# Memory scan: the state products of a step are issued ahead of its output products

## The reference, cut to what matters

```python
def step(state, inp):
    s, n, m = state
    qc, kc, vc, ic, fc = inp
    ...
    qk = jnp.einsum('bhtd,bhsd->bhts', qc, kc) * jnp.exp(dmat - m_t[..., None])
    num = jnp.einsum('bhts,bhsv->bhtv', qk, vc) + w_inter[..., None] * jnp.einsum('bhtd,bhdv->bhtv', qc, s)
    den = jnp.sum(qk, axis=-1) + w_inter * jnp.einsum('bhtd,bhd->bht', qc, n)
    h = num / jnp.maximum(jnp.abs(den), jnp.exp(-m_t))[..., None]
    ...
    kw = kc * jnp.exp(g - m_new[..., None])[..., None]
    s_new = decay[..., None, None] * s + jnp.einsum('bhsd,bhsv->bhdv', kw, vc)
    n_new = decay[..., None] * n + jnp.sum(kw, axis=2)
    return (s_new, n_new, m_new), h
```

## Time and profile before

| | us |
|---|---|
| median of 3 runs | 4023.66 (4020.28 to 4027.84) |
| profiled execution, its time | 4025.71 |
| profiled execution, its span | 4023.7 |
| PE busy | 3649.3 (91% of the span) |
| PEld busy | 2898.3 (72%) |
| DVE busy | 2201.8 (55%) |
| ACT busy | 1558.4 (39%) |
| POOL busy | 1129.1 (28%) |

### The profile page before, as it was taken

The page is one execution under the profiler, slowest core; times in us unless marked ns, Lnnn a source line. Parts: engine busy times, 40 slices in busy tenths (PEclk is TensorE's granted clock), DMA queues, the critical chain, the costliest instruction groups (busy, mean ns, idle before and its releaser), DMA issues. The chain is left out here.

```text
span 4023.7 us, 43905 instructions
## 1 busy us (share of the span) xinstructions
PE 3649.3 (91%) x16690; PEld 2898.3 (72%) x16690; DVE 2201.8 (55%) x2454; ACT 1558.4 (39%) x2064; POOL 1129.1 (28%) x593
## 2 busy tenths in 40 slices
PE   4899997587899999979889899999798999999997
PEld 1778886465687878766677667777676888888886
DVE  7467635655788888856656322222245543353338
ACT  3321233344677777734322222222222333232234
POOL 2231222035211111133331212122143444444443
PEclk8899998788899999969999999999999999999999
DMA  4412135655899999944421312111253323222333
GB/s 158 122 37 75 68 113 168 222 172 200 325 402 398 402 397 402 397 183 157 150 105 53 124 46 69 52 65 61 89 184 139 123 90 99 95 94 97 98 110 126
DMA packets 174817, 650.33 MB, mean 162 GB/s; under 512 B 21376, under 2 KB 55008, under 8 KB 158528
## 3 DMA queue, kind: packets, MB, share of 16 engines
q1 hardware_dynamic: 135424, 555.34, 38.1%
q10 hardware_dynamic: 28864, 60.87, 4.0%
q0 software_dynamic: 10368, 31.91, 2.1%
HBM read 540.71 MB, written 107.34 MB: 161 GB/s over the span
## 5 line engine op out<-in xcount | busy, mean ns | idle before, releaser
L3625 POOL TENSOR_TENSOR t_wl<-t_raw,t_wh 128x1024 fp32r<-128x1024 f32 x160 | 386.4, 2416 | 522.5 <-ACT t_wh L3671 522.3
L100 PE MATMUL m_b<-b_high,m_high 128*128 128x512 f32 x960 | 404.9, 422 | 10.7 <-POOL m_low L2498 8.1
L102 PE MATMUL m_b<-b_high,m_low 128*128 128x512 f32 x960 | 382.1, 398 | 0.0
L101 PE MATMUL m_b<-b_rest,m_high 128*128 128x512 f32 x960 | 381.8, 398 | 0.0
L2496 POOL TENSOR_TENSOR m_high<-m_raw,m_one 128x1024 fp32r<-128x1024 f32 x60 | 120.6, 2010 | 788.5 <-PE m_b L102 723.1
L100 PE MATMUL t_b<-b_high,t_wh 128*128 128x512 f32 x768 | 302.0, 393 | 15.2 <-POOL t_wl L3625 15.2
L102 PE MATMUL t_b<-b_high,t_wl 128*128 128x512 f32 x768 | 299.7, 390 | 0.0
L101 PE MATMUL t_b<-b_rest,t_wh 128*128 128x512 f32 x768 | 299.6, 390 | 0.0
L3671 ACT ACTIVATE t_wh<-t_raw 128x1024 fp32r<-128x1024 f32 x160 | 169.1, 1057 | 312.7 <-PE t_b L102 292.4
L100 PE MATMUL zs_z<-zs_hs,zs_high 128*128 128x512 f32 (+1 forms) x584 | 226.6, 388 | 27.9 <-POOL zs_hs L279 27.9
L100 PEld LDWEIGHTS m_b<-b_high,m_high 128*128 128x128 f32 x960 | 184.8, 193 | 64.4 <-issue 11.3
(11 more groups left out here) (647 smaller groups left out, 8774.4 us busy)
## 6 DMA issues: line engine op xcount, KB each, us to landing
moe_raw<-in_expert_w SPq DMA_DIRECT2D x79, 2048.0 KB, 10.2
ex_raw<-in_expert_w SPq DMA_DIRECT2D x39, 2048.0 KB, 10.7
t_raw<-in_w_ff SPq DMA_DIRECT2D x128, 512.0 KB, 3.4
m_raw<-in_w_ug SPq DMA_DIRECT2D x60, 512.0 KB, 4.6
yrows<-ex_y ACTq DMA_DIRECT2D x38, 512.0 KB, 11.1
zs_raw<-in_ada_w SPq DMA_DIRECT2D x32, 512.0 KB, 4.7
gates<-m_ob SPq DMA_DIRECT2D x32, 512.0 KB, 2.8
me_g<-gates SPq DMA_DIRECT2D x32, 512.0 KB, 4.0
```

The source lines that it names most:

```text
L100: nc.tensor.matmul(out, w[0], x[0], start=first, stop=False)
L101: nc.tensor.matmul(out, w[0], x[1], start=False, stop=False)
L102: return nc.tensor.matmul(out, w[1], x[0], start=False, stop=last)
L3625: self.nc.gpsimd.tensor_tensor(self.wl[u % self.NW][:], self.raw[u % 2][:], self.wh[u % self.NW][:].bitcast(F32), ALU.subtract).then_inc(s ...
```

## The change

In `Memory.tensor` the loop of the 8 state products, with its waits on `kw_done`, moves ahead of the block of the output products. The wait on `updated` stays ahead of both. Nothing is added or removed, and the programs of DVE, ACT, POOL and SP are the same.

```diff
             pe.wait_ge(self.updated, 3 * n)
+            for d in range(2):
+                pe.wait_ge(self.kw_done[d], n + 1)
+                for h, out in enumerate(self.four(self.X[d], self.EX, d)):
+                    mm = mm_(out, self.kw[d][:, h, :], self.v[:, ORDER[d][n], h, :], start=True, stop=True)
+                mm.then_inc(self.stepped, 1)
             if i >= 0:
                 for d in range(2):
                     pe.wait_ge(self.q_in[d], i + 1)
@@
                         mm = mm_(out, self.inter[d][i % 2][:, h, :], self.state[:, d, h, :], start=False, stop=True)
                     mm.then_inc(self.o_done, 1)
-            for d in range(2):
-                pe.wait_ge(self.kw_done[d], n + 1)
-                for h, out in enumerate(self.four(self.X[d], self.EX, d)):
-                    mm = mm_(out, self.kw[d][:, h, :], self.v[:, ORDER[d][n], h, :], start=True, stop=True)
-                mm.then_inc(self.stepped, 1)
             Z.multiply(pe, fills[n][1])
```

## The result

The changed kernel takes 4033.27 us (median of 12 runs, 4029.78 to 4037.76) against 4025.15 us (12 runs, 4020.28 to 4032.62): a ratio of 1.0021, 95% interval 1.0012 to 1.0029. It is slower by 8.1 us, where 6.5 was forecast. That is just at the bound of 0.2%, with the interval on both sides of it; the forecast gave "no change" 0.64 and "slower" 0.32. One profile of each kernel shows the scan more sharply than the times do. In programs with the same code up to there, the starts of steps 2 to 5 repeat to 0.05 us. From step 6 on they don't: there the same code took up to 3 us more or less, mostly by its clock. And the stretch behind the scan, whose code is never changed, took between 3248.7 and 3254.6 us in the fourteen profiles, so the times carry a scatter that has nothing to do with the scan.

A forecast was written before the change was run, and what follows sets the result against it. PE was busy 91% of the span, but the change was priced from the engines' waits in the scan's steps. 0.9 + 1.8 - 2.1 + 5.4 + 0.5 = +6.5 us on the median 4023.66 gave 4030.2, range 4023 to 4037.

The forecast's parts named there:

- The cost is the delay of the last output: Steps with outputs: the last output comes 1.79 us later where PE reached it without a wait; earlier state products help nobody.
- two regimes: Steps 2 to 4 are bound by PE's work, 18.98 us each; from step 5 the chain crosses engines and delays pass on.
- Steps 2 to 4, +0.9: PE's key transposes wait for DVE's late state update, 0.3 us in each of three steps; bounds 0 to 1.5.
- Step 5, +1.8: The output delay of 1.79 us passes undiminished through DVE's mask, ACT's copy, SP's queue and the tile's DMA.
- DVE's idle time in front of L374: Step 5, a sign to look for in the changed kernel's profile: this idle time about 1.8 us longer.
- POOL's price of nothing: Step 5: POOL's splitting holds two other DVE instructions just as long, so the sum is unchanged; bounds -1 and +1.
- Step 6, -2.1: State products fill PE's 3.23 us hole, outputs keep full clock, DVE starts 0.6 us late instead of 2.7; bounds -3.7 to +0.2.
- Steps 7 to 9, +5.4 and 0.5: Three output delays of 1.79 us come through, plus 0.25 us each in steps 7 and 8 for a later clock rise.
- The sum: Whole kernel: all terms together +6.5 us, 4030.2 us against the median, 0.16% slower.
- A: Rival, slower for sure: step 6's outputs stay at half clock and give nothing back; +9.8 us, time 4033.5; chance 0.27.
- C: Rival, faster: DVE's state update waits for the state products, so earlier ones shorten the scan; chance 0.04.
- B: Rival, nearly nothing: step 6 returns 3.7, steps 2 to 4 lose nothing, clock kinder in steps 7 to 9; +2.0; chance 0.19.

The follow-up runs named there:

- other waits behind: Changed order on PE plus tiles loaded first on SP and the embedding unit copied first on ACT, against the kernel before: ratio 0.9990, scan 222.99 us.
- the run with the loads first: Old order on PE; SP loads two modulation tiles ahead of the last projection tile's stores, against the kernel before: ratio 0.9982, scan 216.16 us.
- the doubled products: Old order; in step 6 the state products also run an extra time ahead of the outputs' wait, against the kernel before: ratio 1.0002, scan 225.75 us.
- the runs with steps 7 to 9: State products first in steps 7, 8 and 9 only, against the kernel before: ratio 1.0015, scan 232.09 us.
- early copy: Old order on PE; in steps 7 and 8 ACT copies the first embedding unit ahead of its decays, against the kernel before: ratio 0.9996, scan 221.57 us.
- all steps but 6: State products first in every step except step 6, against the kernel before: ratio 1.0020, scan 230.90 us.
- step 6 alone: State products first in step 6 only, old order elsewhere, against the kernel before: ratio 1.0000, scan 225.63 us.

## Why the prediction was right, step by step

- **The cost is the delay of the last output.** Right. It is 1.77 us in step 2, for 1.79 forecast, and what was to come earlier, the state products, shortens no wait. All seven steps and their two regimes were as described, and the cost with other waits behind shows that it isn't tied to them.
- **Steps 2 to 4, +0.9.** Mechanism right, size 1.2: 0.40 a step instead of 0.3. The slack was read well, for the stall in front of the transposes is 0.27 us. What the sum left out is that the transposes behind it run 0.09 us longer.
- **Step 5, +1.8.** Right up to SP's queue: the denominators of step 5 are 2.97 late, SP's tile loads begin 2.96 late (101.41 against 98.45 us of the scan), the tile lands 2.6 late, and so are the keys of step 6 (115.38 against 112.79). The run with the loads first shows that queue to be the cause. One sign of the prediction failed: DVE's idle time in front of L374 was to grow by 1.8 us and shrank from 10.55 to 10.17. It could not grow, since DVE and the tile are delayed alike. POOL's price of nothing was right, but by luck. The prediction let POOL move by 0.9 and DVE by 2.7, so that L374 would be held in place of L1073. POOL's pair moved by 2.54, nearly as much as DVE, and held the same L1073 for the same 5.13 us.
- **Step 6, -2.1.** The start of DVE came out almost exactly (0.51 late, forecast 0.6; that is -2.5), and the doubled products show the clock as the cause. But the term was meant to reach the end, and did not: DVE then lost 1.8 us to POOL. I had bounded that collision only as a gain of 1.6 where DVE would get clear of POOL, and not asked what else stands in POOL's way when DVE comes earlier relative to it. It came 2.2 us earlier relative to it, since POOL's last pair moved by 2.67 and not by 0.9. With POOL at +0.9 only the second of the pair would have met DVE, and the way to the mask would have been some 4.4 us instead of 5.82 (an estimate: POOL's L472 began at 128.41 of the scan before, plus 0.9, and takes 2.36). From step 5 (2.97) to step 7's keys (140.98 against 138.70, 2.3 late) 0.7 was given back, not 2.1, and 0.4 of it by the tile in front of step 6. By the times, the kernel with the old order in step 6 is not slower than the changed one (1.0020 and 1.0021).
- **Steps 7 to 9, +5.4 and 0.5.** +6.1 alone, so the size is right. In the changed kernel's profile it was 4.2, from 2.3 to 6.5, since step 7 passed on only 0.4: its fills ran less of their time at half clock (0.80 as the mean between its keys and its denominators, before 0.73), and PE waited 0.80 us for the modulation there instead of 1.15. Windows over the fills' first part, before and then after:

```profile
692.40:699.00 6.60, 6.60 (x20) 5.54 (x21) 3.86 (x6) 0.60 (x1) 0.00 (x0) 0.51 0.64 201
```

```profile
694.00:700.00 6.00, 6.00 (x22) 4.84 (x22) 3.11 (x5) 1.20 (x2) 0.00 (x0) 0.72 0.81 225
```

- **The sum.** +6.5 against +6.7 in the profile is closer than its terms: step 6 was 1.4 short, steps 2 to 4 0.3, and step 7 gave 1.3 back, mostly by the clock. That these cancel is luck: in other runs the same stretch of step 7 gave up to 3 us or nothing. The median of 12 runs says 8.1 (4.8 to 11.7 by the interval). Whether the 1.4 us between are the profiles' luck with the clock or chance of the times, these runs can't say. The forecast time, 4030.2, stood on a median of three runs (4023.66) that twelve runs put 1.5 us higher.
- **The rivals.** A, in which step 6 gives nothing back, is nearer to the truth for that step, and by another way than its own: the clock did rise, but DVE lost the gain to POOL. C had no source, as argued. B's kinder clock came in step 7.

## What to carry to other kernels

When two independent groups of work share an engine, ask which result has the earlier reader and how long that reader works before it wants the other: here DVE works 5 us on the outputs before it touches the state products, so the outputs go first. To put work into a hole in front of a wait is free only for the hole; if that hole exists in one step of eight, the other seven pay. And a gain of time on one engine has to be followed to the next point where two engines meet, with the shift of both: the 2.5 us won on PE in step 6 ended on an instruction of POOL, which had moved more than was thought. A total that comes out as forecast doesn't show that its terms did.

## What the runs showed of the hardware that I had not expected

- Three DVE instructions, one on 128x8 elements and two on 128x4, 0.17 us and 0.36 for the two by themselves, took 1.53 and 2.39 us while POOL's 128x1024 instructions ran, and ended with them. With those cut to 8 columns all three took their usual time.
- Programs that are the same up to step 6 reach its denominators at 128.68, 128.63 and 126.86 us of the scan (before, and the runs with steps 7 to 9 and with the early copy), mostly by how long the clock stays at 1.2 GHz in the outputs (they took 5.2 us in the last, 6.7 in the others). With the hole filled it was 127.27 and 127.15, so the filled hole doesn't beat the luckiest run; two runs are too few to say that it removes the spread.
- Behind a small hole the clock fell too. In the run with all steps but 6, PE stood still for 1.11 us in front of step 6's outputs and began them at clock 1.00; 1.3 us on it fell to 0.50 although PE never stopped, and they took 5.3 us. With products in the hole (0.92, 1.52 and 1.59 us of it left, in the changed kernel, the run with the doubled products and that with step 6 alone) it stayed at 1.00.
- Where PE had just waited for DVE's update (0.16 us booked, and none in the next step, where it began 0.27 later all the same), four transposes took 0.66 us instead of 0.60, in a stretch whose clock is 1.00.
